# Where the small unit's scatter is issued and where its token codes are made, in a decoder step with a mixture of experts

## What is computed

```python
x = x + g1 * (mixed @ w_out)                    # the last eight items of the dense part
h2 = rms_norm(x, norm2_g) * (1 + sc2) + sh2
g_sel = argmax(h2 @ w_rg + b_rg)                # one of 4 groups
top_v, top_i = top_k(e_in, 2)                   # 2 of its 8 experts
y = sum(gate * ((silu(xb @ w1[e]) * (xb @ w3[e])) @ w2[e]))
x = x + g2 * y
y_prompt, y_sample = rms_norm(x), rms_norm(x)
```

## Time and profile before

| | us |
|---|---|
| median of three runs | 1599.64 |
| lowest and highest of them | 1598.01, 1600.19 |
| the profiled execution's own time | 1598.65 |
| its span, first to last instruction | 1596.9 |
| TensorE busy | 1543.2 (97% of the span) |
| VectorE busy | 1243.0 (78%) |
| ScalarE busy | 796.2 (50%) |
| GpSimd busy | 371.7 (23%) |

### The profile page before, as it was taken

How to read it: one execution, slowest core, us unless ns; L and a number is a source line. 1 busy time by engine, 2 the same in 40 slices (tenths; PEclk the granted TensorE clock), 3 DMA queues, 4 the chain that set the end, 5 groups by cost and what they waited for, 6 DMA issues and landing times.

```text
span 1596.9 us, 23207 instructions
## 1 busy us (share of the span) xinstructions
PE 1543.2 (97%) x9054; PEld 1319.0 (83%) x9054; DVE 1243.0 (78%) x1707; ACT 796.2 (50%) x879; POOL 371.7 (23%) x274
## 2 busy tenths in 40 slices
PE   5999999999999999999999999899999999999994
PEld 3777788878889999999999995688888888888882
DVE  4668887756747888886655548899999999999995
ACT  4222232235333223323242246678778877887775
POOL 2311000000000000002000202346665455445531
PEclk9999999999999999999999999999999999999997
DMA  9966222425334323233422567999999999999975
GB/s 334 325 195 195 85 80 86 146 80 155 119 93 148 118 82 91 67 94 86 129 80 81 175 214 280 410 392 390 399 397 375 388 375 377 386 387 389 387 278 228
DMA packets 218993, 362.90 MB, mean 227 GB/s; under 512 B 19351, under 2 KB 167927, under 8 KB 193786
## 3 DMA queue, kind: packets, MB, share of 16 engines
q1 hardware_dynamic: 196588, 323.10, 56.1%
q0 software_dynamic: 21648, 36.14, 7.8%
q10 hardware_dynamic: 646, 2.15, 0.3%
HBM read 362.64 MB, written 32.08 MB: 247 GB/s over the span
## 4 chain that ended last, share of the span: by engine, by line
PE 87%; DVE 5%; DMA 3%; issue 1%; ACT 1%; DVEq 1%; SPq 1%; POOL 0%; POOLq 0%; ACTq 0%
PE z L3123 16%; PE z L3125 16%; PE z L3124 16%; PE z L962 7%; PE z L964 7%; PE z L963 7%; PE z L981 3%; PE z L980 3%; PE z L979 3%; PE q L3014 2%; PE q L951 2%; DMA ada<-in_w_ada_dram 1%; DVE wl L1397 1%; DVE conv L2491 1%; PE q L3033 1%; PE q L970 1%
## 5 line engine op out<-in xcount | busy, mean ns | idle before, releaser
L1397 DVE TENSOR_TENSOR wl<-wr,whr 128x2048 fp32r<-128x2048 f32 x190 | 428.5, 2283 | 0.0
L3123 PE MATMUL z<-h_hi,w_hi 128*128 128x272 f32 (+1 forms) x1248 | 406.7, 326 | 2.3 <-DVE h_lo L2310 1.8
L3125 PE MATMUL z<-h_hi,w_lo 128*128 128x272 f32 (+1 forms) x1248 | 402.5, 323 | 0.0
L3124 PE MATMUL z<-h_lo,w_hi 128*128 128x272 f32 (+1 forms) x1248 | 401.3, 322 | 0.0
L726 ACT ACTIVATE whr<-wr 128x2048 fp32r<-128x2048 f32 x190 | 359.7, 1911 | 51.9 <-PE z L964 51.1
L2310 DVE TENSOR_TENSOR w_lo<-w_raw,w_hi 128x1024 fp32r<-128x1024 f32 (+1 forms) x168 | 179.4, 1068 | 128.8 <-ACT w_hi L2005 128.8
L3123 PEld LDWEIGHTS z<-h_hi,w_hi 128*128 128x128 f32 x1248 | 234.7, 188 | 28.3 <-issue 7.4
L3125 PEld LDWEIGHTS z<-h_hi,w_lo 128*128 128x128 f32 x1248 | 234.4, 188 | 16.6
L3124 PEld LDWEIGHTS z<-h_lo,w_hi 128*128 128x128 f32 x1248 | 234.8, 188 | 15.8 <-issue 0.2
L2491 DVE SCALAR_TENSOR_TENSOR conv<-a_in,parT,conv 128x512 f32<-128x512 f32 x360 | 193.7, 582 | 14.5 <-issue 1.3
L962 PE MATMUL z<-whr,xTh 128*128 128x512 f32 x512 | 203.1, 397 | 0.0
(11 more groups left out here) (522 smaller groups left out, 2309.0 us busy)
## 6 DMA issues: line engine op xcount, KB each, us to landing
wr<-in_w_dram SPq DMA_DIRECT2D x198, 1024.0 KB, 7.6
w_raw<-in_w_in_dram SPq DMA_DIRECT2D x104, 512.0 KB, 3.8
ada<-in_w_ada_dram SPq DMA_DIRECT2D x6, 2048.0 KB, 14.0
w_raw<-in_w_branch_dram SPq DMA_DIRECT2D x48, 256.0 KB, 2.7
w_raw<-in_w_out_dram SPq DMA_DIRECT2D x16, 512.0 KB, 4.1
ada_h<-in_w_ada_dram SPq DMA_DIRECT2D x2, 2048.0 KB, 15.3
ada_u<-in_w_ada_dram SPq DMA_DIRECT2D x2, 2048.0 KB, 9.9
ada_m<-in_w_ada_dram SPq DMA_DIRECT2D x2, 2048.0 KB, 10.9
```

What stands on the lines that cost most here:

```text
L1397: return dve.tensor_tensor(out, a, b, op)
L3123: pe.matmul(out, w_hi[w][:, k, :], hi[:, k, t0:t1], start=(k == 0), stop=False)
L3124: pe.matmul(out, w_hi[w][:, k, :], lo[:, k, t0:t1], start=False, stop=False)
L3125: last = pe.matmul(out, w_lo[w][:, k, :], hi[:, k, t0:t1], start=False, stop=(k == kn - 1))
```

## The change

Two moves. On GpSimd the scatter of `first_y`, with its wait, goes ahead of `gather(3)`. On TensorE the eight small matmuls go from between `out_item(1, 0, 1)` and `out_item(1, 1, 0)` to behind `out_item(1, 1, 0)`; and on VectorE a single copy of both code columns to SBUF, which frees `q[1]`, stands right behind `out_smp(1, 0)`, ahead of the next `w_lo`, while the rest of `first_tokens` reads the copy.

```diff
             pool.dma_start(g2p[:], ...).then_inc(g2_in, 16)
+            pool.wait_ge(first_tok_ok[0], first_tok_ok[1] + 2)
+            pool.indirect_dma_start(x1_dram.rearrange("t (h d) -> (t h) d", h=2), ...
+                                    ).then_inc(first_sc[0], 16)
             for b in range(NB):
                 if b + 3 < NB:
                     gather(b + 3)
...
                     gate_gather(0, g2_in)
-                    pool.wait_ge(first_tok_ok[0], first_tok_ok[1] + 2)
-                    pool.indirect_dma_start(x1_dram.rearrange("t (h d) -> (t h) d", h=2), ...
-                                            ).then_inc(first_sc[0], 16)
...
                 def first_tokens():
-                    s = q_wait_ready(dve, "first")
-                    dve.tensor_copy(code[:], q[s][:, 0, 0:1])
                     dve.tensor_scalar(upper[:], vlo[:], float(P - XR), None, ALU.is_lt)
                     dve.drain()
-                    dve.scalar_tensor_tensor(code[:], q[s][:, 0, 1:2], float(P), code[:], ALU.mult, ALU.add).then_inc(q_free[s], 1)
+                    dve.scalar_tensor_tensor(code[:, 0:1], code[:, 1:2], float(P), code[:, 0:1], ALU.mult, ALU.add)
...
                     out_smp(j, 0)
+                    if g and j == 1:
+                        s = q_wait_ready(dve, "first")
+                        dve.tensor_copy(code[:], q[s][:, 0, 0:2]).then_inc(q_free[s], 1)
                     ahead(g, O0 + 2 * j)
...
                 out_item(g, 0, 1)
-                if g:
-                    s = q_wait_free(pe, "first")
-                    pe.wait_ge(first_ok[0], first_ok[1] + 2)
...
-                    last.then_inc(q_ready[s], 1)
                 for j in range(1, KD // 2):
...
                     out_item(g, j, 0)
+                    if g and j == 1:
+                        s = q_wait_free(pe, "first")
+                        pe.wait_ge(first_ok[0], first_ok[1] + 2)
...
+                        last.then_inc(q_ready[s], 1)
                     if j < KD // 2 - 1:
                         out_transpose(g, j - 1, 0)
```

## The result

| | before | after |
|---|---|---|
| median of four runs, us | 1599.56 | 1588.25 |
| lowest and highest | 1598.01, 1600.19 | 1587.35, 1589.34 |
| the profiled execution's own time | 1598.65 | 1588.35 |
| its span | 1596.9 | 1586.5 |

The ratio is 0.9936 with a 95% interval from 0.9922 to 0.9949: the changed kernel is faster by about 10.2 us (8.2 to 12.5). The forecast was 1591.6 us in a range from 1587.5 to 1595.3, with a chance of 0.90 for faster. Sign and range hold. By the medians the change gave 11.3 us where 8.0 were forecast, 3.3 us more; by the ratio, 2.2 us more. The median of before was 1599.64 over three runs, and is 1599.56 with a fourth.

A forecast was written before the change was run, and what follows sets the result against it. The prediction took TensorE to be the bound, each wait costing idle time plus half clock behind it. Token codes 6.0 us plus scatter 1.4 us made 7.4 us: 1591.2 or 1592.2 by base, forecast 1591.6 us, range 1587.5 to 1595.3.

The forecast's parts named there:

- Part one: Token codes, behind item (1, 0): TensorE goes on 3.35 us earlier and 2.65 us of half clock return, 6.0 us.
- Part two: Scatter moved earlier, wait at `G(1)`: TensorE 1.9 us earlier, less 0.5 us for the clock, 1.4 us (0.9 to 3.7).
- So `result(0)` moves only from 1029.68 to 1027.1: VectorE ahead of `G(1)`: `result(0)` also needs `gfac`, which ends at 1027.07, so TensorE gains 1.9 us, not 6.35.
- If the return stays at 1037.4, 5.5 us are worked at half clock: Clock behind `G(1)`: 2.75 us lost in that case, against 1.8 before; the middle, 2.3 us, was taken.
- All of it should reach the end: After 1037: the summed 7.4 us reach the end, as TensorE hardly idles and `whr` never waited for a load.
- the second wait goes whole: Rival at `G(1)`, 5%: gate rows land sooner and TensorE never stops, 8.15 us there, 14.2 in all, 1584.5 us.
- The first fall stays: Rival behind item (1, 0), 6%: the clock still falls, so 3.35 us there, sum 4.75, 1594.2 us.
- The first gain is eaten: Rival before the blocks, 8%: a last output item waits for `w_hi`, losing up to 6.0 us, 1595.2 to 1598.0 us.
- The scatter holds up the weights: Rival in the weight loads, 3%: the earlier scatter delays them, costing 3.4 us at most, 1603.0 us.

The follow-up runs named there:

- copy_only: Kernel before with only VectorE's copy of the codes moved ahead of `w_lo`; small matmuls and scatter left in place: 1593.44 us, ratio 0.9968.
- mm_only: Kernel before with only the eight small matmuls moved behind item (1, 0); VectorE still reads the codes behind `w_lo`: 1599.19 us, ratio 0.9999.
- fill_first: Kernel before with sixteen unread matmuls of 272 columns added in TensorE's wait for `q[1]`: 1596.41 us, ratio 0.9983.
- scatter_only: Kernel before with only the scatter of `first_y` moved ahead of `gather(3)`: 1594.44 us, ratio 0.9973.
- scatter_between: Kernel before with only the scatter of `first_y` moved, to behind `gather(3)` and ahead of `gate_gather(0)`: 1596.46 us, ratio 0.9979.
- swap_load: Kernel before with GpSimd's direct load of `g2p` put ahead of `gather(2)`: 1598.49 us, ratio 1.0000.
- split_load: Kernel before with the load of `first_g` made by four DMAs of 32 partitions in place of two of 64: 1599.79 us, ratio 1.0004.
- codes_only: Changed kernel with the scatter put back behind `gate_gather(0)`, leaving the token-code moves alone: 1593.02 us, ratio 0.9965 to the kernel before.
- gate_early: Changed kernel with `gate_index` made by VectorE in block 0 ahead of the first `gate()`: 1584.26 us, ratio 0.9908 to the kernel before.
- fill_second: Changed kernel with ten unread matmuls of 512 columns added ahead of `G(1)`: 1586.98 us, ratio 0.9924 to the kernel before.
- gate_early_late_scatter: Changed kernel with `gate_index` made early in block 0 and the scatter back behind `gate_gather(0)`: 1586.27 us, ratio 0.9921 to the kernel before.

## Why the prediction was right, and where it was not

**Part one was right by its steps.** Forecast: TensorE goes on 3.35 us earlier and 2.65 us of half clock come back. Measured in the two profiles: 3.39 and 2.75. The wait was forecast at 1.3 us and ended by the copy; it is 1.28. `copy_only`, `mm_only` and `fill_first` show the three terms apart (the copy's place, the matmuls' place, the clock). One reservation belongs to the size of the clock's term: the profile of before had the clock low for 6.8 us there. The 6.8 us stand in that profile alone. In `scatter_only`, `scatter_between`, `swap_load`, `split_load` and `mm_only`, with waits of 3.6 to 4.6 us at the same place, it was low for 3.4 us. The 2.75 us are thus the upper end, and 5.6 us for the whole part, as timed in `codes_only`, is a better size than the 6.1 of the two profiles.

**Part two had the right chain and two terms of the wrong size.** The step "So `result(0)` moves only from 1029.68 to 1027.1" and the links behind it, `gfac` and then `whr(18)`, are in the trace as forecast. The gain in the wait was 2.18 us for a forecast 1.9, and the wait that was left 4.17 for 4.4. The scatter took 13.3 us to land where 11.07 were assumed, which cost nothing, since it still landed 16 us before `gfac`. The term that was mis-sized is "If the return stays at 1037.4, 5.5 us are worked at half clock". The return didn't stay: the clock was low for 3.4 us in place of 6.8, TensorE worked 3.2 us at half clock in place of 3.6, and a forecast loss of 0.5 us became a gain of 0.16. Together part two gave 2.34 us in place of 1.4, in its range of 0.9 to 3.7. By the Trainium skill (TensorE: Matmul & The Clock Gate, What's actually happening) the count of slow matmuls differs from run to run, and the prediction took both lengths for draws. At the first place that agrees with the 6.8 and 3.4 us found there. At the second it was no draw in these runs: low for 6.8 us in the seven profiles with a wait of about 6.4 us, and for 3.4 us in the five with 2.0 to 4.2.

**The end was not in the sum at all.** "All of it should reach the end" was argued from the weights, and held: stretch *B* hasn't moved by 0.02 us. But behind the last block 1.83 us more were gained, by the drain. The prediction priced the scatter's issue, its landing and the queue behind it, and had no term for GpSimd's closing drain: it put the end of the run at nothing. For this term it was luck that the time still lies in the range: it is 0.75 us above the lower bound, and that bound was half a microsecond wider than the terms of the range give with the spread of the runs added (1588.0 to 1594.2, where 1587.5 to 1595.3 was stated).

The working closes: 7.4 forecast, 1.0 more in *A*, 1.8 in *D*, and from the two executions themselves 0.7 in *C* less 0.6 ahead of `sig`; 10.3 us between the two profiled executions.

**The rivals.** That the second wait goes whole didn't happen: with the scatter away from behind them the gate rows still took 7.4 us from the end of their issue (1012.72) until ScalarE's wait for them ended, where it was 7.7 before. Early gate rows were made in `gate_early`, and there the wait does go; its gain was 3.2 us of *A* over the changed kernel. That is less than the 4.17 us of the wait because that profile had the clock low for 3.4 us from 965.8 on, where the changed kernel's had not; counted from behind that place, from TensorE's wait of 0.9 us in the small unit near 982 to the second `gfac`, it gained 4.85 us. The first fall stays: no, the clock is 1.00. The first gain is eaten: no, though the row of `w_lo` shows VectorE waiting 1.68 us for `w_hi`, 0.78 more than before, so part of the slack was used. The scatter holds up the weights: no. In the first blocks TensorE has no wait of over 1 us apart from `G(1)`.

## What to carry to other kernels

Free a shared buffer with a copy the moment it is readable, ahead of any long step on the same engine: here 0.15 us of copy ahead of a step of 1.2 us was worth 5 us, because the copy ended TensorE's wait 2.4 us sooner and kept its clock from falling. When a stall has two causes that end within a few us of each other, removing the later buys only the distance between them (2.2 of 6.35 us); follow the chain to the second cause, and move that too (`gate_early`, about 4 us more). Read the last microseconds of a run as closely as the longest stall: an engine's closing drain can be on the path, and it can depend on something that happened 600 us before.

## What the runs showed of the hardware that was not expected

- GpSimd's closing DRAIN takes 8.36 to 8.46 us in nine profiles and 5.99 to 6.03 us in five, with nothing between. It is short where one adding scatter of 256 KB is issued ahead of a gather of 512 KB some 590 us before, and long where it comes behind it. It is worth 1.8 us of the run's time.
- Idle time of 1.28 and 1.62 us left TensorE's clock at 1.00; 3.56 us and more brought it down every time. With 2.00 us of idle time (`fill_second`) it fell 0.8 us after TensorE had gone back to work.
- The clock was low for 3.4 us or for 6.8 us near these places, never for another length. In `swap_load` it fell at 970.4 with no wait of over 0.3 us in the microseconds ahead, in a stretch of small matmuls, and `split_load`, with the same work there, kept it. The stretches of `swap_load` and then of `split_load`:

```profile
969.00:972.00 3.00, 3.00 (x16) 2.16 (x16) 2.76 (x22) 1.54 (x3) 0.00 (x0) 0.73 1.01 404
```

```profile
969.00:972.00 3.00, 3.00 (x13) 1.83 (x14) 2.64 (x26) 2.05 (x2) 0.00 (x0) 1.00 1.03 373
```

  That fall, at 965.8 to 971.0, came in six of the fourteen profiles: `swap_load`, `fill_first`, `scatter_between`, `scatter_only`, `gate_early` and `gate_early_late_scatter`. From TensorE's wait of 0.8 us for `ot` at the end of the dense part to its wait of about 0.9 us in the small unit, 28 us later, the six took 29.4 us and the eight others 27.7 or 27.8 (958.59 to 987.94 in `swap_load`, 957.96 to 985.72 in `split_load`). So it costs 1.6 to 1.7 us there, and stretch *A* of one profile must be compared with that of another with this in mind; of the 1.6 us between those two, 1.3 are left at the end of *A*.
